# Attention: new key rows turned by VectorE in blocks of 32 and stored in runs of 128 bytes by the sync queue, in place of TensorE transposes

## The reference, cut to what matters

```
qkv = (h @ w_qkv).reshape(nb, L, N_ATTN_GROUPS, 3, ATTN_HEADS, ATTN_HEAD_DIM)
for g, (window, dil) in enumerate(ATTN_PATTERNS):
    q, k, v = qkv[:, :, g, 0], qkv[:, :, g, 1], qkv[:, :, g, 2]
    o, lam = band_attention(to_strided(q, dil), to_strided(k, dil), to_strided(v, dil), window // dil)
    keep = min(window, L)
    rows.append(jnp.stack([k, v], axis=2)[:, L - keep:])
```

## Time and profile before

| | |
|---|---|
| median of 3 runs | 1665.72 us (1664.75 to 1667.55) |
| the profiled execution's own time | 1667.31 us |
| its span (first to last instruction) | 1665.2 us |
| PE busy | 1624.9 us, 98% of the span |
| DVE, ACT, POOL busy | 622.4, 442.6, 132.9 us |
| DMA | 538.03 MB, mean 323 GB/s |
| attention's projections begin, end | 786.9, 1133.4 us |

### The profile page before, as it was taken

The page is one execution under the profiler, slowest core; times in us unless marked ns, Lnnn a source line. Parts: engine busy times, 40 slices in busy tenths (PEclk is TensorE's granted clock), DMA queues, the critical chain, the costliest instruction groups (busy, mean ns, idle before and its releaser), DMA issues.

```text
span 1665.2 us, 21571 instructions
## 1 busy us (share of the span) xinstructions
PE 1624.9 (98%) x8171; PEld 957.4 (57%) x8171; DVE 622.4 (37%) x1359; ACT 442.6 (27%) x1151; POOL 132.9 (8%) x278
## 2 busy tenths in 40 slices
PE   8999989999999999999999999999999999999997
PEld 7888867653444344344877888867653444344342
DVE  3689993321222132223023554553421322222123
ACT  3477762211111111112143142232311111111112
POOL 1212231100000000001001202320000000000000
PEclk9999999999999999999999999999999999999999
DMA  9557676499999999999344947687499999999994
GB/s 343 197 177 222 211 230 265 147 400 407 427 428 427 428 428 429 428 428 395 126 139 154 341 166 252 180 253 313 159 401 409 428 427 428 428 428 429 428 427 191
DMA packets 101670, 538.03 MB, mean 323 GB/s; under 512 B 7996, under 2 KB 32772, under 8 KB 76722
## 3 DMA queue, kind: packets, MB, share of 16 engines
q1 hardware_dynamic: 85910, 485.20, 72.1%
q0 software_dynamic: 15360, 51.30, 9.7%
q10 hardware_dynamic: 316, 0.37, 0.1%
HBM read 520.61 MB, written 16.42 MB: 322 GB/s over the span
## 4 chain that ended last, share of the span: by engine, by line
PE 78%; DVE 10%; DMA 7%; ACT 3%; issue 2%; SPq 0%; DVEq 0%; ACTq 0%
PE bank L973 23%; PE bank L1353 14%; PE bank L985 12%; DMA ring<-in_moe_w_gate_up 6%; PE bank L957 5%; PE bank L838 5%; PE bank L979 4%; PE bank L1278 3%; PE bank L1250 3%; DVE arena L2377 2%; PE bank L1582 2%; DVE arena L2226 2%; PE bank L999 1%; ACT arena L1697 1%; DVE arena L2385 1%
## 5 line engine op out<-in xcount | busy, mean ns | idle before, releaser
L973 PE MATMUL bank<-ring,arena 128*64 128x512 f32 x1520 | 336.1, 593 | 6.1 <-DMA ring<-in_moe_w_gate_up 6.0
L1353 PE MATMUL bank<-hT,ring 128*128 128x264 f32 x1152 | 268.7, 389 | 0.0
L1353 PEld LDWEIGHTS bank<-hT,ring 128*128 128x128 f32 x1152 | 214.6, 190 | 40.0 <-issue 3.9
L973 PEld LDWEIGHTS bank<-ring,arena 128*64 128x64 f32 x1520 | 112.0, 137 | 217.7 <-issue 217.4
L2226 DVE TENSOR_TENSOR arena<-arena,bank 128x512 f32<-128x512 f32 x32 | 34.3, 1072 | 392.8 <-ACT arena L1697 392.8
L985 PE MATMUL bank<-ring,arena 128*64 128x512 f32 x768 | 170.1, 595 | 1.6 <-DVE arena L2147 1.6
L979 PE MATMUL bank<-arena 128*128 128x512 f32 x256 | 126.9, 618 | 1.6 <-ACT arena L1707 1.6
L1697 ACT ACTIVATE arena<-bank 128x512 f32<-128x512 f32 x32 | 19.1, 597 | 391.3 <-PE bank L973 391.3
L2173 DVE SCALAR_TENSOR_TENSOR arena<-arena 128x1024 f32<-128x1024 f32 x32 | 41.1, 1285 | 213.1 <-ACT arena L1707 213.1
L973 PE MATMUL bank<-arena 128*64 128x512 f32 x512 | 112.6, 592 | 0.0
L985 PEld LDWEIGHTS bank<-ring,arena 128*64 128x64 f32 x768 | 53.8, 137 | 101.8 <-issue 99.7
(11 more groups left out here) (342 smaller groups left out, 1740.4 us busy)
## 6 DMA issues: line engine op xcount, KB each, us to landing
ring<-in_moe_w_gate_up SPq DMA_DIRECT2D x94, 2048.0 KB, 18.7
ring<-in_moe_w_down SPq DMA_DIRECT2D x48, 2048.0 KB, 22.9
arena<-in_moe_w_gate_up SPq DMA_DIRECT2D x32, 2048.0 KB, 18.1
ring<-in_attn_qkv SPq DMA_DIRECT2D x18, 2048.0 KB, 11.8
arena<-in_moe_w_down SPq DMA_DIRECT2D x16, 2048.0 KB, 22.5
ring<-in_ssm_in_proj SPq DMA_DIRECT2D x10, 2048.0 KB, 14.0
out<-arena POOLq DMA_DIRECT2D x24, 512.0 KB, 4.0
arena<-in_cache_kv_w POOLq DMA_DIRECT2D x20, 512.0 KB, 7.7
```

The lines of the kernel that those rows point to most:

```text
L973: mm = pe.matmul(bank[j][e * SLOTS:(e + 1) * SLOTS, :], Xg[:, 4 * half + k, 2 * (p % 2) + e, :], gate_rows(2 * half + e, p, k, first)[:, j ...
L1353: mm = pe.matmul(bank[i % 2][:, 0:T], wv[:, k, (i % 4) * P:(i % 4 + 1) * P], hT[:, k, :], start=(k == 0), stop=(k == DT - 1))
```

## The change

A k tile is no longer transposed by PE or copied by ACT. VectorE turns each tile's 256 prompt columns in blocks of 32 by 32 in place of the block: what was channel 32e + j of token 32b + i lies afterwards on partition 32e + i, column 32b + j, in the same buffer `KV` (seen as `KVF`). So a partition holds, for one token of each block of 32, 32 consecutive channels. SP stores that with four DMAs a tile (one for each block e of 32 partitions): each has 32 partitions by 8 token blocks (4 at g = 0) of 32 elements, 128 bytes. A group has 8 VectorE instructions and 32 DMAs of 32 KB (16 KB at g = 0).

The semaphores `s_xld` and `s_vld` count the stores of tiles 0 to 3 and 4 to 7, `s_stc` the turned tiles. POOL keeps the values' stores and the samples' own rows; the keys' own rows are now job 1, in the place where the k tile's last job was (step 0 of the values' stage).

```diff
+            def keys_out(g, q):
+                lo = 1 if g == 0 else 0
+                rows = kv_p[g][0, 0, :, 0].rearrange("(b i) h d -> i b (h d)", i=BLK)
+                for t in range(4 * q, 4 * q + 4):
+                    sp.wait_ge(s_stc, 3 + DT * g + t + 1)
+                    for e in range(4):
+                        have = KVF[e * BLK:(e + 1) * BLK, t, lo * P:TP].rearrange("i (b j) -> i b j", j=BLK)
+                        at = t * P + e * BLK
+                        sp.dma_start(rows[:, :, at:at + BLK], have).then_inc(s_vld if q else s_xld, 16)
             for n in range(ATT_CHUNKS):
+                if n % RING == 2 and n > RING:
+                    keys_out(n // RING - 1, 0)
+                elif n % RING == 3 and n > RING:
+                    keys_out(n // RING - 1, 1)
...
+            keys_out(2, 0)
+            keys_out(2, 1)
             moe_stream(1, attention_done)
```

```diff
-                    kind, t = (j - 1) // DT, (j - 1) % DT
-                    pe.wait_ge(q_e, 24 * g + 8 + 8 * kind + t + 1)
-                    src = vT[:, t % 2, :] if kind else kT[:, t, :]
+                    t = j - 2
+                    pe.wait_ge(q_e, 24 * g + 16 + t + 1)
...
                     if t == 0:
-                        if kind:
-                            act.wait_ge(kvst, 96 * g + 48)
-                        elif g:
-                            act.wait_ge(kvst, 96 * g)
-                            act.wait_ge(h_v, DT * g)
+                        act.wait_ge(kvst, KVST[g + 1] - 48)
+                        act.wait_ge(s_xld, KEYS_EARLY[g + 1])
+                        act.wait_ge(s_vld, KEYS_LATE[g + 1])
...
-                    rows_job(g, t)
+                    if t == 0:
+                        if g == 0:
+                            pe.wait_ge(c_v, 1)
+                        rows_job(g, 0)
```

VectorE:

```diff
+            def keys_turned(g):
+                if g:
+                    v.wait_ge(kvst, KVST[g])
+                    v.wait_ge(h_v, DT * g)
+                for t in range(DT):
+                    v.wait_ge(q_e, 24 * g + 8 + t + 1)
+                    v.transpose(KVF[:, t, :], kT[:, t, 0:TP]).then_inc(s_stc, 1)
...
                     cache_scores(u)
+                keys_turned(g)
                 own_scores(g)
```

More of the change, by code:

```diff
@@ L55 @@
 VSLOTS = 5
-JOBS = 1 + 2 * DT
+JOBS = 2 + DT
+BLK = 32
 CJOBS = [(g, b, 1) for g in range(2) for b in range(NS)] + [(2, b, 2) for b in range(0, NS, 2)]
@@ L287, in bass_hybrid_step @@
         deep = [sem(f"extra_weights{l}_landed") for l in range(2)]
-        s_xld = sem("x_landed")
-        s_vld = sem("vectors_landed")
+        s_xld = sem("x_landed_then_early_keys_stored")
+        s_vld = sem("vectors_landed_then_late_keys_stored")
         s_aux = sem("step_loads_then_half_chunks_landed")
@@ L306, in bass_hybrid_step @@
         s_stp = sem("conv_state_transposed")
-        s_stc = sem("conv_state_columns")
+        s_stc = sem("conv_state_columns_then_keys_turned")
         s_dtp = sem("dt_projected_then_sums_turned")
@@ L451, in value_rows @@
             return ring[:, slot, at:at + 2 * D].rearrange("p (j d) -> p j d", j=2)
+        KEYS_EARLY = [32 + 256 * g for g in range(NGRP + 1)]
+        KEYS_LATE = [112 + 256 * g for g in range(NGRP + 1)]
+        KVST = [64 * g for g in range(NGRP + 1)]
+        KVF = KV.rearrange("p c (t n) -> p (c t) n", n=TP)
         def lane(g, c):
@@ L825, in _ @@
                             cached_values(m)
-                    for q in range(2):
-                        pool.wait_ge(kv_e, JOBS * g + 1 + DT * kind + 4 * q + 4)
+                    pool.wait_ge(kv_e, JOBS * g + 2)
+                    for q in range(2 * kind):
+                        pool.wait_ge(kv_e, JOBS * g + 2 + 4 * q + 4)
                         pool.dma_start(rows[:, :, kind, 512 * q:512 * q + 512],
@@ L830, in _ @@
                     pool.dma_start(own_rows[kind], kv_own).then_inc(kvst, 16)
-            pool.wait_ge(kvst, 96 * NGRP)
+            pool.wait_ge(kvst, KVST[NGRP])
+            pool.wait_ge(s_xld, KEYS_EARLY[NGRP])
+            pool.wait_ge(s_vld, KEYS_LATE[NGRP])
         @block.tensor
@@ L1368, in rows_job @@
                     mm = pe.matmul(own, own_c, ident[:, :], start=True, stop=True)
-                else:
-                    kind, t = (j - 1) // DT, (j - 1) % DT
-                    pe.wait_ge(q_e, 24 * g + 8 + 8 * kind + t + 1)
-                    src = vT[:, t % 2, :] if kind else kT[:, t, :]
+                elif j == 1:
+                    pe.wait_ge(c_a, 2 * g + 2)
+                    mm = pe.matmul(own, own_c, ident[:, :], start=True, stop=True)
+                else:
+                    t = j - 2
+                    pe.wait_ge(q_e, 24 * g + 16 + t + 1)
                     for c in range(2):
-                        mm = transpose(bank[7][:, c * P:(c + 1) * P], src[:, lane(g, c)])
+                        mm = transpose(bank[7][:, c * P:(c + 1) * P], vT[:, t % 2, lane(g, c)])
                     if t == DT - 1:
-                        if kind == 0:
-                            pe.wait_ge(c_a, 2 * g + 2)
-                        mm = pe.matmul(own, vTs[:, g, :] if kind else own_c, ident[:, :], start=True, stop=True)
+                        mm = pe.matmul(own, vTs[:, g, :], ident[:, :], start=True, stop=True)
                 mm.then_inc(kv_t, 1)
@@ L1443, in values @@
                 pe.wait_ge(h_c, 2 * n + 2)
-                pe.wait_ge(kv_e, JOBS * g + 1 + DT + t + 1)
+                pe.wait_ge(kv_e, JOBS * g + 2 + t + 1)
                 if n >= 1:
@@ L1535, in lagging @@
                 if s <= DT:
-                    rows_job(g, 8 + s)
+                    rows_job(g, 1 + s)
                 if g and 1 <= s <= DT:
@@ L1863, in copy_tile @@
                         act.wait_ge(c_v, 1 + g)
-                        act.wait_ge(kv_t, JOBS * (g - 1) + 1 + DT)
+                        if i:
+                            act.wait_ge(s_stc, 3 + DT * g)
                     dst = (qT if i < DT else kT)[:, i % DT, :]
@@ L1869, in copy_tile @@
                     if t >= 2:
-                        act.wait_ge(kv_t, JOBS * g + 1 + DT + t - 1)
+                        act.wait_ge(kv_t, JOBS * g + 2 + t - 1)
                     elif g:
@@ L1891, in copy_rows @@
                     act.activation(q_own, own, ACT.Copy).then_inc(kv_e, 1)
+                elif j == 1:
+                    if g:
+                        act.wait_ge(kvst, KVST[g])
+                    act.activation(kv_own, own, ACT.Copy).then_inc(kv_e, 1)
                 else:
-                    kind, t = (j - 1) // DT, (j - 1) % DT
+                    t = j - 2
                     if t == 0:
-                        if kind:
-                            act.wait_ge(kvst, 96 * g + 48)
-                        elif g:
-                            act.wait_ge(kvst, 96 * g)
-                            act.wait_ge(h_v, DT * g)
+                        act.wait_ge(kvst, KVST[g + 1] - 48)
+                        act.wait_ge(s_xld, KEYS_EARLY[g + 1])
+                        act.wait_ge(s_vld, KEYS_LATE[g + 1])
                     if t == DT - 1:
@@ L1937, in lagging @@
                 if s <= DT:
-                    copy_rows(g, 8 + s)
+                    copy_rows(g, 1 + s)
                 if g and 1 <= s <= DT:
@@ L1961, in _ @@
                     copy_tile(g, DT + t)
-                    copy_rows(g, t)
+                    if t == 0:
+                        copy_rows(g, 0)
                 own_columns(g, 1)
@@ L2040, in expert_buffers @@
                 if l:
-                    v.wait_ge(kvst, 96 * NGRP)
+                    v.wait_ge(kvst, KVST[NGRP])
+                    v.wait_ge(s_xld, KEYS_EARLY[NGRP])
+                    v.wait_ge(s_vld, KEYS_LATE[NGRP])
                 v.sem_inc(s.act, 1)
@@ L2609, in _ @@
             variance(4, 2, NS)
-            v.wait_ge(s_vld, 128)
+            v.wait_ge(s_vld, KEYS_LATE[NGRP] + 16)
             for i, t in enumerate(NORM_ORDER[4]):
```

3 lines of the change are left out of this document (1 added, 2 removed).

## The result

The changed kernel takes 1692.05 us (median of 4 runs, 1689.10 to 1695.09), the kernel before 1666.63 (1664.75 to 1670.76): ratio 1.0149, 95% interval 1.0131 to 1.0166. It is slower by 25.4 us. The forecast had the sign, the place and, in group 2, the mechanism, and half the size: 13.0. The measured time lies above its own range of 1670 to 1690.

The account below looks back on a forecast made before the run. PE's stream in attention was taken as the bound, with the experts following one to one; +0.8 (group 1) and +12.2 (group 2) made +13.0, 1680.3 us own time, 1678.7 for the median, range 1670 to 1690 (wider: 1663 to 1704).

Parts of the forecast that it names:

- The row jobs' 0.23 us: PE, k and values' stages: each k row job removed saves 0.23 us, 1.9 a group, 5.7 in all.
- SP's pitch: SP's queue: key-store issues 0.47 us apart, so a group's 32 cost 15.0 us.
- DVE's transposes: DVE: eight block transposes a group at 0.42 us each, 3.4 us in one block in groups 1 and 2.
- The mechanism of group 2: Group 2: engines alternate packets of key stores and cached values whatever their size; keys 13.0 us late, shift +12.2.
- Rival 1: Group 2: several small packets go in a turn, so cached values don't hold up stores; +3.7, 1669.4 us; chance 0.20.
- rival 2: Both late groups: a key DMA costs 1.0 us; 1703 us, or about 1712 with turn-taking; chance 0.15.
- rival 3: Groups 1 and 2: SP's pitch under 0.38, no turn-taking, keys land before needed; -4.4, 1661.3 us; chance 0.12.
- 15.0, 0.4 (chunk 14's issue), 2.6 (landing): Group 1: 32 store issues, chunk 14 charged its issue alone, then landing; keys copied at 976.0 against 975.5, shift +0.8.
- a small one in group 1: ACT in group 1: a small wait for the key stores, against some 13 us in group 2 and none in group 0.
- 0.3 for PE to find its pace: PE behind the waits at step 2 in groups 1 and 2: restarting costs 0.3 us each.
- -1.1, since PE's wait for the cached values is swallowed: PE in group 2: its wait for the cached values at 1095 disappears inside the longer wait, giving back 1.1 us.
- The masked scores of step 0 are 3.4 late; PE has one step of slack there: Groups 1 and 2, behind DVE's transposes: scores 3.4 us late, but PE has one step of slack.

Follow-up runs that it names:

- values_behind_keys: Changed kernel, but POOL issues group 2's cached values only once all key stores have landed: 1682.91 us, 1.0089 of the kernel before.
- chunk_behind_stores: Changed kernel, but both halves of a group's key stores are issued ahead of chunk 14 (and 8): 1689.28 us, 1.0131 of the kernel before.
- pe_kept_busy: Changed kernel with unread matmuls of constants filling PE's waits ahead of step 2's row job in groups 1 and 2: 1694.38 us, 1.0149 of before.
- no_key_stores: Changed kernel without the 96 key-store DMAs; ACT waits for the transposes alone: 1666.40 us, 0.9986 of the kernel before.
- no_stores_no_turns: Changed kernel without the 96 key stores and without DVE's 24 block transposes: 1665.42 us, 0.9982 of the kernel before.
- last_job_later: Changed kernel with transposes between DVE's cached key jobs and group 2's last cached job behind step 0's masked scores: 1666.07 us, 0.9984 of before.

## Why the forecast had the sign and half the size

**Held.** The row jobs' 0.23 us is gone from PE: 1.6 a k stage as forecast (tiles 24, 40 and 64), and 5.2 in all, forecast 5.7, since the part in the values' stages is 0.0 to 0.2 a group and not 0.3. Group 0 is hidden. SP's pitch was 0.49 alone, forecast 0.47 (0.52 in group 1 without the chunk between, 16.53 / 32). DVE's transposes came in one block of 2.7 us, 0.40 one and 0.34 apart, forecast 0.42 each. The first store of group 1 was issued 167.0 us after tile 1, forecast 166.5 (957.2 + 0.4 - 791.1); that it is so near is luck, since the forecast took half of a gain of 0 to 4.9 us. In group 2 it came at 287.3; the forecast's 1071.8 was to move with PE, 280.7 + 6.5 = 287.2. It does move with PE, but the agreement to 0.1 us is luck again, since the queries' way ahead of it takes 11.6 to 14.3 us by the trace. The mechanism of group 2, one packet of each queue in turn, is shown by values_behind_keys and by the packets of the two queues (705 and 707). Rival 1 (no hold-up by the cached values) and rival 2 (dear small writes) are refuted by it, rival 3 by the two waits.

**Terms that were mis-sized.** Measured, from the timelines above:

```
                                                    forecast  measured
group 1: keys late at step 2's row job                +0.5      +4.7
group 1: PE's way from there to the next tile         +0.3      +1.8
group 2: keys late at step 2's row job               +13.0     +14.6
group 2: PE's way from there to the next tile         +0.3      +2.7
group 2: cached values' wait and the rest             -1.1      +0.4
sum                                                  +13.0     +24.2
```

(Group 1: 984.53 - 795.49 = 189.04 against 975.48 - 791.10 = 184.38. Group 2: 1111.56 - 795.49 = 316.07 against 1086.08 - 791.10 = 294.98, less the 6.5 of group 1.)

**The step that failed** is the price of chunk 14 in group 1, where the forecast had +0.8 and +6.5 came; the restart of PE is nearly as large a miss.

*Group 1, the step "15.0, 0.4 (chunk 14's issue), 2.6 (landing)".* I had chunk 14 cost its issue alone. It is 2 MB in the same queue, with half of the keys behind it, and the 32 issues and it took 20.3 us instead of 15.4; chunk_behind_stores gives 3.8 of these 4.9 back. From the end of the last issue to ACT's copy it took 1.3 us and not 2.6. I had seen this chunk in its effect on DVE's operands, and not on the stores behind it. This is the largest miss, 4.2 us (4.7 for 0.5). The prediction looked for "a small one in group 1" of ACT's waits; it was 11.69 us.

*The restart, "0.3 for PE to find its pace".* After waits of 7.9 and 15.1 us the granted clock was 0.50, and the row job ran at 1.2 GHz. It cost 1.8 and 2.7 us, 3.9 more than I had. pe_kept_busy has the full clock and still needs 3.8 us for the way in group 2, so 1.7 of the 2.7 is the clock (1.4 of 1.8 in group 1). Of the other 1.0 the timeline shows 0.4 as a wait for DVE inside the row job; most of the rest is the row job's first six products, 1.21 us long where six take 0.83 elsewhere. That the clock's part is worth anything to the whole kernel wasn't shown: the timed ratio didn't move.

*Group 2, the turns.* First issue to ACT's copy was 28.3 us, forecast 26.9 (1071.8 to 1098.7): 1.4 of the 1.6 is here. The step, one packet of each queue in turn, was right, but its numbers were off and made up for one another in part. The DMA view of the changed kernel from 1091.25 to 1108.4 holds all packets of the cached values:

```profile
q0 software_dynamic: 1344, 4.75, 85.4%
q1 hardware_dynamic: 3143, 0.38, 15.4%
```

They began 8.5 us behind the issue of the first store, forecast 10.8 (1082.6 - 1071.8), when 16 key DMAs had still to go and not 9. They lasted 17.0 us, forecast 12.9, since they were 84 packets an engine and not 72 and had more keys beside them. What followed up to ACT's copy took 2.8, forecast 3.2.

*"-1.1, since PE's wait for the cached values is swallowed".* It stands unchanged at 1123.71, 1.09 us, by issue (1095.05 in the earlier trace rows). Nothing had been gained there.

**Something the sum had not.** "The masked scores of step 0 are 3.4 late; PE has one step of slack there" was wrong: no_key_stores shows a PE wait of 1.97 us on them. In the changed kernel 1.0 of it is seen (tile 64 +4.9, tile 66 +5.9), and it is hardly a term of its own there, since the stores' end decides at tile 67. As soon as the stores are hidden it decides: a cost of up to 3.1 us (no_key_stores against no_stores_no_turns) out of 5.2.

**What stays open.** Why the queries' way in group 2 took 2.6 us longer in chunk_behind_stores than in the changed kernel, by the edit or by chance. Why values_behind_keys, whose group 1 is that of the changed kernel, has +8.0 there and not +6.5: 1.2 of the 1.5 is seen, as its first store goes out 0.5 us later (167.5 after tile 1) and its 32 issues and the chunk take 21.0 us instead of 20.3, but not what makes them so. And the 1.56 us that PE still waits for DVE at step 2 in last_job_later, where DVE works without a gap from 1081.3 until it releases PE at 1085.4. No run was made for any of them.

## What to carry to other kernels

Small stores whose end somebody waits for belong as early as their data allow, spread out, and neither behind a big chunk in their own queue nor beside another queue's burst: the same 96 stores made the kernel 25 us slower in blocks behind DVE's other jobs, and between them cost nothing that the timed runs could tell. When work moves from the engine that bounds the kernel to one with 37% busy time (DVE, the page after), look at what stands behind the spot where it is put: a block of 2.7 us on it took back some 3 of the 5.2 us saved. And a wait of PE is to be priced with its restart: here 1.8 and 2.7 us on top.

## What the runs showed of the hardware

- A store in runs of 128 bytes cost the DMA engines 12.0 ns a packet (40.9% of 16 x 7.0 us for 3808 packets, completion writes among them); beside chunk 14, 14.9 (96.6% of 16 x 8.0 = 123.6 us, less 1024 chunk packets at 87 ns, over 2316), near the load's 14.5 in the earlier trace rows. The Trainium skill, DMA: Bandwidth & Descriptors, section Specifications, has a read-modify-write below 512 bytes. Whether one is in these times no run shows: 128 bytes in 12.0 ns is 10.7 bytes a ns, where the chunk's packets had 23.5 (2048 / 87). It did not set the pace, since a key DMA kept an engine busy for 17 x 12.0 ns = 0.20 us and SP took 0.49.
- SP's own issue of one store took 0.49 us with its queue alone on the engines, 0.70 behind chunk 14 and 3.2 beside the cached values. In the changed kernel's group 2 two issues took 0.84 us together before the cached values came, and three took 9.69 beside them, 3.2 each:

```profile
1082.79 0.84 SPq L591 DMA_DIRECT2D out<-arena  x2
...
1095.92 9.69 SPq L591 DMA_DIRECT2D out<-arena  x3
```

- A block transpose of 128x256 on DVE took 403 ns, about what the copy of the same columns takes (0.42 in the earlier trace rows), and eight in a row are 0.34 apart; in the view of its line (shortest, median, longest, in ns):

```profile
L2493 DVE STREAM_TRANSPOSE arena<-arena x24: 401/403/446, 824.8 to 1084.6; 128x256 f32<-128x256 f32 x24
```
